# Second experts: which gathers stand behind which unit, and what stands between the last weights and behind the branch

## The reference

```python
def hier_moe(x, rg_w, rg_b, re_w, re_b, w_gate, w_up, w_down):
    ...
    g_star = jnp.argmax(lg, -1)
    ...
    top_v, top_i = lax.top_k(le, TOP_K_IN_GROUP)
    w_sel = jax.nn.softmax(top_v, -1)
    ...
    for g in range(N_GROUPS):
        h = jax.nn.silu(jnp.einsum('td,edf->tef', t, w_gate[g])) * jnp.einsum('td,edf->tef', t, w_up[g])
        y = y + jnp.einsum('tef,efd->td', h * gate[:, g, :, None], w_down[g])
```

## Time and profile before

| | us |
|---|---|
| median of 3 runs (1661.5 to 1667.85) | 1662.71 |
| the profiled execution, its own time | 1661.5 |
| its span | 1659.6 |
| TensorE busy | 1409.5 (85%) |
| VectorE busy | 509.7 (31%) |
| ScalarE busy | 314.5 (19%) |
| second experts, layer 0 and layer 1, about | 932 to 1175 and 1400 to 1641 |

### The profile page before, as it was taken

The page is one execution under the profiler, slowest core; times in us unless marked ns, Lnnn a source line. Parts: engine busy times, 40 slices in busy tenths (PEclk is TensorE's granted clock), DMA queues, the critical chain, the costliest instruction groups (busy, mean ns, idle before and its releaser), DMA issues.

```text
span 1659.6 us, 19035 instructions
## 1 busy us (share of the span) xinstructions
PE 1409.5 (85%) x7528; PEld 781.9 (47%) x7528; DVE 509.7 (31%) x1140; ACT 314.5 (19%) x659; POOL 0.2 (0%) x4
## 2 busy tenths in 40 slices
PE   6999997856656756789999899988799998999876
PEld 3665785412211211266678544333567686434323
DVE  5225553101101101025753422212247634222213
ACT  2422212000000000113322312111123323122102
POOL 0000000000000000000000000000000000000000
PEclk8999998978878788799999899989899999999988
DMA  9465339999999999972231689999414214899993
GB/s 377 163 249 209 146 153 416 428 428 427 427 428 428 427 428 427 428 314 102 102 126 36 268 367 408 411 418 414 204 60 194 102 51 166 357 408 416 418 412 130
DMA packets 56386, 492.62 MB, mean 297 GB/s; under 512 B 6240, under 2 KB 6624, under 8 KB 25952
## 3 DMA queue, kind: packets, MB, share of 16 engines
q1 hardware_dynamic: 56144, 491.15, 72.3%
q10 hardware_dynamic: 144, 0.13, 0.0%
HBM read 490.21 MB, written 1.05 MB: 296 GB/s over the span
## 4 chain that ended last, share of the span: by engine, by line
PE 61%; DMA 25%; DVE 5%; SPq 5%; issue 2%; ACT 1%; DVEq 0%; ACTq 0%
DMA A<-ring_d 21%; PE PS L636 19%; PE PS L1489 8%; SPq L3114 5%; PE PS L1518 4%; PE PS L980 4%; DMA A<-ranked_d 4%; PE PS L1353 3%; PE PS L641 3%; PE PS L1469 3%; PE PS L1535 2%; PE PS L930 2%; PE PS L1342 1%; PE PS L1179 1%; PE PS L1306 1%
## 5 line engine op out<-in xcount | busy, mean ns | idle before, releaser
L636 PE MATMUL PS<-A 128*128 128x256 f32 (+6 forms) x1592 | 383.1, 398 | 4.5 <-DMA A<-ring_d 2.6
L980 PE MATMUL PS<-A 128*32 128x512 f32 x1536 | 242.5, 769 | 138.2 <-DMA A<-ring_d 137.8
L636 PEld LDWEIGHTS PS<-A 128*128 128x128 f32 (+1 forms) x1592 | 283.0, 196 | 97.8 <-issue 60.0
L1489 PE MATMUL PS<-A 128*64 128x512 f32 (+1 forms) x1024 | 196.0, 633 | 23.7 <-DMA A<-ranked_d 23.5
L980 PEld LDWEIGHTS PS<-A 128*32 128x32 f32 x1536 | 53.0, 126 | 316.1 <-issue 244.6
L1489 PEld LDWEIGHTS PS<-A 128*64 128x64 f32 (+1 forms) x1024 | 58.0, 130 | 142.3 <-issue 140.5
L2018 DVE TENSOR_TENSOR A<-A,PS 128x512 f32<-128x512 f32 x8 | 5.5, 687 | 329.4 <-PE PS L980 329.4
L1518 PE MATMUL PS<-A 128*64 128x512 f32 (+1 forms) x512 | 94.9, 597 | 1.2 <-issue 1.2
L641 PE MATMUL PS<-A 128*128 128x128 f32 (+1 forms) x444 | 69.3, 289 | 25.9 <-DVE A L2018 7.1
L641 PEld LDWEIGHTS PS<-A 128*128 128x128 f32 (+1 forms) x444 | 54.1, 150 | 64.8 <-issue 32.9
L2469 DVE TENSOR_TENSOR A<-A,PS 128x256 f32<-128x256 f32 x26 | 11.0, 423 | 213.0 <-ACT A L3019 213.0
(11 more groups left out here) (356 smaller groups left out, 1278.9 us busy)
## 6 DMA issues: line engine op xcount, KB each, us to landing
A<-ring_d SPq DMA_DIRECT2D x156, 2048.0 KB, 23.4
A<-ranked_d SPq DMA_DIRECT2D x72, 1024.0 KB, 16.3
A<-ranked_d SPq DMA_DIRECT2D x144, 512.0 KB, 15.3
A<-ring_d SPq DMA_DIRECT2D x2, 1312.0 KB, 20.2
A<-ring_d SPq DMA_DIRECT2D x2, 1280.0 KB, 21.3
A<-p_d SPq DMA_DIRECT2D x1, 1232.0 KB, 19.0
A<-xT_d SPq DMA_DIRECT2D x1, 1024.0 KB, 5.5
A<-cT_d SPq DMA_DIRECT2D x1, 1024.0 KB, 11.9
```

The lines of the kernel that those rows point to most:

```text
L636: ins = g.matmul(out, l, r, start=n == 0, stop=n == len(pairs) - 1)
L980: ins = g.matmul(ps[32 * e:32 * e + 32, :], rows_of(kk, e), wv[:, kk % 2, e, :], start=kk == 0, stop=kk == 7)
L1489: ins = g.matmul(ps[m * s:m * s + m, :], XS2[u % 2][:, kk, c:c + m], wv[:, kk % nk, s, :], start=kk == 0, stop=kk == 7)
```

## The change

1. Head of a layer: `expert_gather(0, 1)` moves from ahead of unit 0 to between the two blocks of unit 0, and `gate_up` waits for the gathered rows step by step and not a block at a time. On DVE the comparisons that sort the experts (`by_count`) and those for the other groups (`other_groups`) move behind the first rows.
2. `slots(1)` and both halves of `group_gather(1, ...)` move from behind units 0 and 1 to behind unit 2, and both parts of `expert_gather(2, ...)` behind unit 3.
3. Tail of a layer: in round 12 `group_sum(9)`, `down(10)`, `turned(11)` and the share of group 2 stand between the four blocks of unit 12. `down(12)` goes behind the branch. Of the ring's blocks, `down(10)`'s comes ahead of the fourth block of unit 12 (B43 and B44 trade places).
4. `down` of a four-expert unit waits for its two blocks one at a time; for that the down weights are laid out by halves of the output columns in place of halves of the hidden width. The bytes are the same.

```diff
@@ gathers_behind, rows_behind @@
     if x == 0:
-        return [(j // 2 + 1, j % 2)]
+        return ([(1, 0)], [(1, 1)], [], [(2, 0), (2, 1)])[j]
...
-SHARES, FLAG_AT = (8, 11, 13), 10
+SHARES, FLAG_AT = (8, 11), 10
+LAST = NU - 1
+
+
+def rows_behind(n):
+
+    x, j = UNITS[n]
+    return ([], [], [0, 1], [])[j] if x == 0 else [j] if j < 2 and x < 3 else []
@@ experts_pe @@
-                    for d in range(part * nk // 2, (part + 1) * nk // 2):
-                        g.wait_ge(*at("xs2", l, u, d // 2, d % 2))
+                    if (n, part) == (0, 1):
+                        expert_gather(0, 1)
+                    if n == LAST:
+                        among_last(part)
                     arrived(i)
                     for kk in range(nk * part, nk * part + nk):
+                        if kk % 2 == 0:
+                            g.wait_ge(*at("xs2", l, u, kk // 4, kk // 2 % 2))
...
+            def among_last(part):
+
+                if part == 0:
+                    state["held"] = banks.of["sg", l, LAST]
+                elif part == 1:
+                    group_sum(LAST - 3)
+                elif part == 2:
+                    down(LAST - 2)
+                else:
+                    turned(LAST - 1)
+                    share(2)
+                    state["held"] = None
@@ down @@
-                for w, i in got:
-                    arrived(i)
                 g.wait_ge(*at("hd1", l, n))
                 for half in range(2):
+                    if half == 0 or four(n):
+                        arrived(got[half][1])
...
@@ the loop over the rounds @@
-            expert_gather(0, 1)
             for p in range(NU + 2):
                 if p < NU:
                     x, j = UNITS[p]
                     gate_up(p)
-                    if j == 0 and x < 3:
+                    if p == 0:
+                        state["i"] += 2
+                    if 0 in rows_behind(p):
                         slots(x + 1)
                     if p == 2:
                         turned_norm()
-                    if j < 2 and x < 3:
-                        group_gather(x + 1, j)
+                    for half in rows_behind(p):
+                        group_gather(x + 1, half)
                     for u, part in gathers_behind(p):
                         expert_gather(u, part)
-                if p >= 3:
-                    group_sum(p - 3)
-                if 0 <= p - 2 < NU:
-                    down(p - 2)
-                if 0 <= p - 1 < NU:
-                    turned(p - 1)
+                if p != LAST:
+                    if p >= 3:
+                        group_sum(p - 3)
+                    if 0 <= p - 2 < LAST:
+                        down(p - 2)
+                    if 0 <= p - 1 < NU:
+                        turned(p - 1)
...
             def last_sum():
                 sig.stage = f"e{l}"
-                group_sum(NU - 1)
+                down(LAST)
+                group_sum(LAST)
@@ experts_dve @@
             group_gather(0, 1)
+            expert_gather(0, 0)
+            by_count()
+            expert_gather(0, 1)
             other_groups()
-            expert_gather(0, 0)
-            expert_gather(0, 1)
-            by_count()
```

More of the change, by code:

```diff
@@ L1491, in gate_up, with share @@
                     finished(i)
+            def share(x):
+                for b in range(4):
+                    group_share(g, l, x, b, high("ffn", l, x, b)).then_inc(*full("ffn", l, x, b))
+            def among_last(part):
[9 more added lines that the diff above has]
+                    state["held"] = None
             def turned(p):
@@ L1517, in down @@
                         for s in range(128 // m):
-                            ins = g.matmul(ps[m * s:m * s + m, :], HD[n % 2][:, f, m * s:m * s + m], wd[f][:, s, half * 512:(half + 1) * 512],
-                                           start=f == 0, stop=f == 1)
+                            ins = g.matmul(ps[m * s:m * s + m, :], HD[n % 2][:, f, m * s:m * s + m], wd[half][:, f, s, :], start=f == 0, stop=f == 1)
                     ins.then_inc(*full("ye2", l, n, half))
-                for w, i in got:
-                    finished(i)
+                    if four(n):
+                        finished(got[half][1])
+                if not four(n):
+                    finished(got[0][1])
             def group_sum(p):
@@ L1567, in experts_pe @@
                 if p in SHARES:
-                    for b in range(4):
-                        group_share(g, l, SHARES.index(p), b, high("ffn", l, SHARES.index(p), b)).then_inc(*full("ffn", l, SHARES.index(p), b))
+                    share(SHARES.index(p))
                 if p == FLAG_AT:
@@ L2486, in experts_dve @@
             group_gather(0, 1)
+            expert_gather(0, 0)
+            by_count()
+            expert_gather(0, 1)
             other_groups()
-            expert_gather(0, 0)
-            expert_gather(0, 1)
-            by_count()
             for p in range(NU + 2):
+                if p == LAST:
+                    group_sum(p - 3)
+                    down(p - 2)
+                    for b in range(4):
+                        add_share(v, l, 2, b, out, full)
                 if p < NU:
@@ L2500, in experts_dve @@
                         normed_rows(p - 3)
-                    if j < 2 and x < 3:
-                        group_gather(x + 1, j)
-                        if j == 1:
+                    for half in rows_behind(p):
+                        group_gather(x + 1, half)
+                        if half:
                             places(x + 1)
```

26 lines of the change are left out of this document (13 added, 13 removed).

## The result

The changed kernel takes 1666.9 us in the median of 20 runs (1664.0 to 1673.2), the kernel before on the same chip 1662.65 us (1659.6 to 1667.9). The ratio, taken over runs side by side, is 1.0032 with an interval of 1.0021 to 1.0042; of 1662.65 us that is 5.3 us slower (3.5 to 7.0), where the two medians differ by 4.3. The forecast was 1662.0 us, 0.7 us less than before; its range, 1653 to 1668, holds the time, but the change is a loss, and a clear one, where a small gain was forecast. The profiled execution took 1665.58 us, its span 1663.8 (1659.6 before).

What follows compares the result with a forecast made beforehand. The experts' middle was taken as bound by transfers, the head by TensorE, with a tail after the last block. Layers' -0.2 and -0.5 us gave 1660.8 us, plus 1.2 for the median: 1662.0 us, range 1653 to 1668.

Steps and rivals of the forecast that it cites:

- B21 near 1022: Group 2's first block: SyncE's issue, held by `down(3)` reading B15, would stay near 1022 us despite earlier B10.
- restart of TensorE (B43 lands), behind the head: Tail: TensorE waits for B43, then restarts with `down(10)`, at 1141.5 us in layer 0 and 1610.3 in layer 1.
- half clock at the restart: Tail: clock loss after the idle piece ahead of `down(10)`, taken as 2.0 us in layer 0, 1.6 in layer 1.
- matmuls from there to the branch: Tail: the same work as before less `down(12)`, 22.65 - 3.6 = 19.05 us at full clock.
- gap at the branch: Tail: TensorE's idle time at the branch stays as before, 4.26 us in layer 0, 1.93 in layer 1.
- from `down(12)` to the share's first row: Behind the branch: `down(12)`, `group_sum`, copy and share, with `down(12)` at half clock in layer 0.
- The difference is all the slack: 6.2 - 4.9 = 1.3 us in layer 0, 5.3 - 4.9 = 0.4 us in layer 1: B21's landing time less an empty queue's is its slack; B21 and later blocks move -0.6 us and about 0.
- if it has no slack at all: Upper bound at B21: without slack, the two waits' 0.7 us a layer pass through as loss.
- What comes in are the two waits, 0.7 us: Head, unit 0: matmuls up to `down(3)` are only moved; waits for ACT's rows ahead of B0 and B1 add 0.7 us.
- It costs at least that, at most twice that. I take 2.0 and 1.6: Restart ahead of `down(10)`: half clock costs at least the earlier 1.6 and 1.3 us, at most twice.
- It costs 4.26 us again: Layer 0's branch, reached at 1162.6 us and not hidden behind the last weights, costs TensorE 4.26 us as before.
- Rival 3: Branch meets unfinished transfers, clock stays down longer, head waits pass on; first two alone +5.2 us, 1667.2 us; 1 in 10.

Runs made afterwards that it cites:

- e11: Change's moved group 1 gathers kept, both parts of the first gather ahead of unit 0 again, tail as before; 1660.31 us, 0.997 of the kernel before.
- e4: Changed kernel with `down(12)` ahead of the branch again; 1662.57 us, 0.9989 of the kernel before.
- e9: Changed kernel with `group_sum(11)` moved behind the branch too; 1662.49 us, 0.9992 of the kernel before.
- e2: Tail of the change alone, head in the order of before; 1661.06 us, 0.9998 of the kernel before.
- e8: Changed kernel with head as before, index loads ahead of the slot wait, `down(10)`'s block before quarter three, `group_sum(11)` behind the branch; 1648.89 us, 0.989 of the kernel before.

## Why the prediction was wrong

What it said of the order of things came true: B10 earlier (961.98 us, 31.4 behind the head, before 34.1), B21 near 1022, one idle piece between quarter two and `down(10)` (8.2 us, said 6 to 7, since the prediction put `group_sum(9)` behind quarter two and it stands ahead of it), none from there to the branch, a gap at the branch in both layers, `down(12)` at half clock. From the restart to the branch, without the clock's loss, it said 19.05 us and 19.2 were measured. Its terms were off, and nearly all in one direction, so that a small gain became a loss:

| step, as the prediction put it | said, layers 0, 1 | measured | difference |
|---|---|---|---|
| restart of TensorE (B43 lands), behind the head | 209.4, 210.0 | 211.1, 210.85 | +1.7, +0.85 |
| half clock at the restart | 2.0, 1.6 | 2.75, 2.7 | +0.75, +1.1 |
| matmuls from there to the branch | 19.05 | 19.2 | +0.1, +0.1 |
| gap at the branch | 4.26, 1.93 | 5.71, 3.11 | +1.45, +1.2 |
| from `down(12)` to the share's first row | 11.8, 9.9 | 10.9, 10.0 | -0.9, +0.1 |
| sum | -0.2, -0.5 | +2.9, +2.8 | +3.1, +3.3 |

**"The difference is all the slack: 6.2 - 4.9 = 1.3 us in layer 0, 5.3 - 4.9 = 0.4 us in layer 1"** is the step that failed first. Time to landing less that of an empty queue isn't slack. A transfer that is issued while the last ones drain lands later than one alone, though the queues already move less than they could. Here the GB/s of each microsecond had it: 328 and 287 in layer 0, 328 and 221 in layer 1, where 414 is full. The slack was about zero, so the head's loss went through whole: B47 lands 1.2 us later in both layers, where the step had -0.6 and 0. The upper bound of that step, "if it has no slack at all", was the true case, though with 1.2 us in place of its 0.7.

**"What comes in are the two waits, 0.7 us"**: the two idle rows are 0.34 us each, as said, but `down(3)` starts 1.17 us later in both layers (82.7 behind the head, before 81.6). The 0.5 us between lie in no idle row. e11, without the halves, has `down(3)` at 81.7, so all of it comes with the halves.

**"It costs at least that, at most twice that. I take 2.0 and 1.6"**: 2.75, near the upper bound of 3.1, and 2.7, just above that of 2.6. The rows it was nearest to had idle times of 3.2 us; this one has 8.2. The changed head and tail together have 2.55 to 2.96 us in all eight restarts of four traces (the changed kernel twice, e4 and e9), behind some 8.2 us of idle time, once 6.1. In e2, with the same idle time and the head as before, it was 1.6 and 1.4, so the length of the idle time alone doesn't set it; why the two differ isn't settled.

**"It costs 4.26 us again"** is the step whose mechanism was wrong. I took the gap as the branch's price. It is what is left of a longer one (7.6 us across, 5.0 in layer 1) when the work queued ahead of the branch is used up, and the change took `down(12)` away from there and left `group_sum(11)`. e9 makes the gap smaller than before, 3.22 and 0.54 us, by having `down(11)` last ahead of it. The Trainium skill ("Runtime: NRT & Kernel Launch", Instruction fetch mechanics) has a taken branch out of the window fetch its piece of program. The traces agree in that the crossing is longer in layer 0, where the transfers are full, 7.6 us, than in layer 1, 5.0, and 6.9 us in layer 1 of e8, where they are full as well. The larger gap of the changed kernel in layer 1 isn't that rule's, though: the queues move 11 GB/s there, before 9.

Rival 3, the slower side, priced the same places at +5.2 us: the branch above 3 us in layer 1 (3.11 measured), the clock down for longer, TensorE's loss at the head passed on. It had 1 in 10. That its sum is the measured one is partly luck: it reached its 3 us at the branch by transfers that weren't done, and they had ended. The time across the branch and the GB/s at B21 could both be read before, and would have shown two of its parts to be likely. The forecast instead took for each term the value nearest to no change.

What stays open: why head and tail together cost 7 to 10 us more than apart, and why the head alone, with later blocks, is 3 to 5 us faster than before. The traces put most of it into the clock, of `down(10)` and of the pieces behind the branch, and don't show why it stood at half in one kernel and not in the other.

## What to carry to other kernels

Slack of a transfer is read from the GB/s of the microseconds around it, not from its time to landing: a dip means that there is none, and then everything that its issuing engine does between the wait and the issue is on the path, and belongs ahead of the wait. A fixed delay such as a branch is measured from the start of the last work queued ahead of it, and is longer where transfers are under way; the longest piece that is ready belongs there. Where blocks come from a ring, moving work also moves its block: look at which block it now waits for, and at what that wait keeps waiting behind it.

## What the hardware did that I had not expected

The branch takes TensorE 7.0 to 8.1 us from the start of the last piece with the transfers full (6.9 in e8, layer 1), and 4.5 to 5.6 with them idle, whether that piece takes 1.9 or 3.6 us. TensorE at the restart after 8.2 us idle lost 2.75 us, and 1.4 to 1.6 in a kernel that differs only in the head, some 200 us earlier; with matmuls that nobody reads in that idle time it lost nothing. Eight value loads on SyncE take about 4.4 us, 0.55 us each (the issue comes 4.6 us behind the end of `down(3)` with them and 0.2 us without); those of all groups moved ahead of the wait were worth 0.43% (0.25 to 0.61).
